# Row gathers, search order and the first value block of a product-key expert kernel

## What is computed

```python
q = (xt @ wq).reshape(T, 8, 2, 128)
s = einsum('thpd,hpnd->thpn', q, keys)           # 8 heads, 2 halves, 128 keys
v1, i1 = top_k(s[:, :, 0], 16); v2, i2 = top_k(s[:, :, 1], 16)
sc, ci = top_k(all 256 sums v1 + v2, 16)         # 16 of 16384 experts per head
e = i1[ci // 16] * 128 + i2[ci % 16]; g = softmax(sc)
act = gelu(sum_d x[d] * u_tab[e, d])
out = sum over the 128 chosen e of g * act * v_tab[e]
```

## Time and profile before

| | us |
|---|---|
| median of 3 runs | 2322.4 |
| the profiled execution, its own time | 2329.6 |
| its span, first to last instruction | 2327.8 |
| PE busy | 2186.6 (94%) |
| first score block / first value block starts | 756.6 / 1616.0 |

### The profile page before, as it was taken

The page is one execution under the profiler, slowest core; times in us unless marked ns, Lnnn a source line. Parts: engine busy times, 40 slices in busy tenths (PEclk is TensorE's granted clock), DMA queues, the critical chain, the costliest instruction groups (busy, mean ns, idle before and its releaser), DMA issues.

```text
span 2327.8 us, 34710 instructions
## 1 busy us (share of the span) xinstructions
PE 2186.6 (94%) x11688; PEld 1949.6 (84%) x11688; DVE 1631.0 (70%) x3216; ACT 798.9 (34%) x1028; POOL 771.6 (33%) x522
## 2 busy tenths in 40 slices
PE   5899997999999999898699999997999999999998
PEld 2789996999999878787588989886888888888887
DVE  4449998041343597979878888886777777777785
ACT  1435554112332322222244545443222222222222
POOL 1223322323123567776522222221232222322340
PEclk8999998999799999999899999998999999999997
DMA  8212223334322578787567777776998999889991
GB/s 347 82 56 62 64 64 110 110 102 145 123 64 64 169 240 258 234 270 232 176 215 293 278 278 274 290 276 200 302 307 303 307 309 310 302 307 309 312 319 71
DMA packets 167190, 496.80 MB, mean 213 GB/s; under 512 B 16576, under 2 KB 74304, under 8 KB 165568
## 3 DMA queue, kind: packets, MB, share of 16 engines
q1 hardware_dynamic: 101584, 268.72, 34.9%
q0 software_dynamic: 46080, 167.79, 21.1%
q10 hardware_dynamic: 19440, 59.25, 6.4%
HBM read 433.83 MB, written 61.87 MB: 213 GB/s over the span
## 4 chain that ended last, share of the span: by engine, by line
PE 71%; DVE 12%; issue 8%; DMA 5%; POOL 3%; ACT 2%; SPq 0%; ACTq 0%; POOLq 0%; DVEq 0%
PE P L754 29%; PE P L513 19%; PE P L682 12%; PE P L705 4%; PE P L531 3%; DVE rows L1392 2%; DMA rows<-in_u_tab,Eg 2%; POOL rows L458 2%; DMA gel_scratch<-gel 2%; PE P L599 1%; POOL wLo L442 1%; DMA tb<-in_posT 1%; PE P L726 1%; DVE oh L1421 1%; DVE keysel L1430 1%
## 5 line engine op out<-in xcount | busy, mean ns | idle before, releaser
L778 ACT ACTIVATE wHi<-raw 128x1024 fp32r<-128x1024 f32 x330 | 346.2, 1049 | 1295.2 <-PE P L754 471.7
L682 PE MATMUL P<-hHi,wHi 128*128 128x480 f32 x1024 | 400.4, 391 | 48.4 <-POOL wLo L442 44.6
L754 PE MATMUL P<-wfHi,wHi 128*128 128x480 f32 x1024 | 392.0, 383 | 14.0 <-DVE wfLo L1559 14.0
L682 PE MATMUL P<-hLo,wHi 128*128 128x480 f32 x1024 | 393.2, 384 | 0.0
L682 PE MATMUL P<-hHi,wLo 128*128 128x480 f32 x1024 | 393.0, 384 | 0.0
L754 PE MATMUL P<-wfLo,wHi 128*128 128x480 f32 x1024 | 391.8, 383 | 0.0
L754 PE MATMUL P<-wfHi,wLo 128*128 128x480 f32 x1024 | 391.7, 382 | 0.0
L1491 DVE TENSOR_TENSOR wLo<-raw,wHi 128x1024 fp32r<-128x1024 f32 x188 | 230.2, 1225 | 181.0 <-ACT wHi L778 179.0
L436 POOL TENSOR_TENSOR wLo<-raw,wHi 128x1024 fp32r<-128x1024 f32 (+1 forms) x76 | 186.4, 2454 | 511.9 <-ACT wHi L778 511.7
L458 POOL DMA_INDIRECT rows<-in_v_tab,Eg x160 | 177.4, 1109 | 483.6 <-DVE accB L1531 232.3
L458 POOL DMA_INDIRECT rows<-in_u_tab,Eg x160 | 193.0, 1206 | 393.5 <-DVE rows L1392 359.6
(11 more groups left out here) (216 smaller groups left out, 3164.7 us busy)
## 6 DMA issues: line engine op xcount, KB each, us to landing
raw<-in_ublk SPq DMA_DIRECT2D x128, 512.0 KB, 4.2
raw<-in_v_tab SPq DMA_DIRECT2D x128, 512.0 KB, 5.6
raw<-in_wblk SPq DMA_DIRECT2D x104, 512.0 KB, 3.7
gel_scratch<-gel ACTq DMA_DIRECT2D x128, 240.0 KB, 3.5
gsr<-gel_scratch SPq DMA_DIRECT2D x128, 240.0 KB, 5.7
gate_scratch<-stage ACTq DMA_DIRECT2D x6, 4096.0 KB, 14.5
gates<-gate_scratch SPq DMA_DIRECT2D x32, 768.0 KB, 7.3
modraw<-in_wblk SPq DMA_DIRECT2D x12, 512.0 KB, 13.1
```

The costliest lines, as they stand in the source:

```text
L682: last = nc.tensor.matmul(P[0][:, j % 2, 0:TD], w_[:, j % 2, k * 128:(k + 1) * 128], x_[:, k, C0:T], start=(k == 0 and a == 0 and b == 0), ...
L754: last = nc.tensor.matmul(P[k // 2][:, k % 2, 0:TD], w_[:, j % 2, k * 128:(k + 1) * 128], x_[:, j % 2, :], start=(first and a == 0 and b = ...
L778: return nc.scalar.activation(out, in_, f, **kw)
```

## The change

It has five parts.

1. The ring of `u_tab` rows has eight buffers: four `rows` as before and four `rowsX` in the memory of `x`. So `x` is stored to DRAM (`x_park`, in the unused eighth part of `gate_scratch`) by SP ahead of the load of query block 6, and loaded back to a new place `x2` by SP half-way through the value blocks; the last steps use `x2`. The `v_tab` gathers keep four buffers.
2. `D1` is 88: 88 gathers are spread over the 60 blocks 8 to 67, written out; the other 72 come in loops of 24 with row numbers copied 12 at a time.
3. DVE's units: tiles 0 to 2 of heads 0 to 5, then (6,0), (6,1), (7,0), (6,2), (7,1), (7,2), then tiles 3 and 4. `select` works on some of the heads of a tile (tile 0: heads 0 to 3, 4 to 6, 7; others 0 to 3 and 4 to 7) with up to five dots inside. 70 dots may be done before softmax, 12 after it, 6 around the first `low` on DVE.
4. PE waits for softmax and transposes behind block 63, ACT's exp stands ahead of its last eight blocks.
5. `gsr` and the first buffer of `gates4`, `wf`, `wfHi` and `wfLo` lie in the memory of `x`; SP loads `gsr` and gates of the first value blocks once all `u_tab` dots are done. The gate products of the last score block come ahead of its scores, ACT rounds the first `wf` ahead of the last GELU, and the first value block starts with chunks 4 to 7.

The diff, cut to its core:

```diff
-UR = 4
+UR, VR = 8, 4
-D1 = 80
+D1 = 88
     x = sb("x", [128, KC, T])
     free_to(0)
+    rowsX = sb("rowsX", [128, UR - VR, D])
+    free_to(0)
+    gsr = sb("gsr", [128, 4, TD])
+    gates4 = [sb("gates4a", [128, 6, 4, 64])]
+    wf, wfHi, wfLo = (...)
...
+            if (name, m) == ("wq", 6):
+                sp_.wait_ge(s["norm_t"], 2 * KC)
+                sp_.dma_start(x_park, x[:, :, :]).then_inc(s["x_pk"], 16)
...
-        for j in range(RAW):
-            value_block(0, j)
+        sp_.wait_ge(s["row_free"], NG + UR)
+        sp_.wait_ge(s["x_pk"], 16)
         for h in range(2):
-            sp_.wait_ge(gel_st[h], 16 * NE // 2)
             sp_.wait_ge(gate_st[h], 16 * 3)
+            sp_.wait_ge(gel_st[h], 16 * 2)
         gate_rows(0, 0, 0)
         for j in range(RAW):
             gate_block(0, j)
+        for j in range(RAW):
+            value_block(0, j)
+        sp_.wait_ge(s["prod_done"], P_V)
         gate_rows(0, 1, 4)
+        for h in range(2):
+            sp_.wait_ge(gel_st[h], 16 * NE // 2)
...
+        with sp_.Fori(1, NE // 16) as i:
+            eight_blocks(i)
+        sp_.dma_start(x2[:, :, :], x_park).then_inc(s["x_up"], 16)
+        with sp_.Fori(NE // 16, NE // 8) as i:
+            eight_blocks(i)
...
+        for b in range(U1 - 8):
+            low(0, 0, 8 + b)
+            for g in range(b * D1 // (U1 - 8), (b + 1) * D1 // (U1 - 8)):
+                if g % 8 == 0:
+                    indices(0, 0, g, g // 8 % 2, 0, 8, g // 8 + 1)
+                gather(0, 0, g + 1, g % UR, g // 8 % 2, g % 8, u_tab)
...
-        with pe.Fori(0, U1 // 4) as i:
+        with pe.Fori(0, U1 // 4 - 1) as i:
...
         last.then_inc(s["tr2_done"], 1)
+        for j in range(4):
+            expert_scores(U1 // 4 - 1, 0, j)
...
+        gates_of(U2 // 4 - 1, 3)
+        expert_scores(U2 // 4 - 1, U1, 3)
...
-        with act.Fori(1, U1 // 4 - 1) as i:
+        with act.Fori(1, U1 // 4 - 2) as i:
...
+            if last:
+                value_halves(0, 0)
+                gelu_out(ib, U1, j)
...
-        units = [(h, t) for h in range(4) for t in range(2)] + [(h, 0) for h in range(4, HEADS)]
-        units += [(h, 1) for h in range(4, HEADS)] + [(h, t) for t in range(2, NT) for h in range(HEADS)]
+        units = [(h, t) for h in range(6) for t in range(3)] + [(6, 0), (6, 1), (7, 0), (6, 2), (7, 1), (7, 2)]
+        units += [(h, t) for t in range(3, NT) for h in range(HEADS)]
...
             search(n, unit, before)
-                early_dots(3)
+            early_dots(2)
+            if before is not None:
+                hb, tb_ = before
+                parts = {3: [(0, 4)], 6: [(4, 7)], 7: [(7, 8)]} if tb_ == 0 else {7: [(0, 4), (4, 8)]} if tb_ < 3 else {
+                    3: [(0, 4)], 7: [(4, 8)]}
+                for h0, h1 in parts.get(hb, ()):
+                    select(tb_, h0, h1)
+                    selects += 1
+                if hb == HEADS - 1 and tb_ < 2:
+                    row_numbers(tb_, selects)
+                    if tb_ == 0:
+                        dve.sem_inc(s["row_free"], UR)
+                        dotted[1] = D1 - 18
+                elif n < len(units):
+                    early_dots(1)
...
                         ).then_inc(s["sm_ready"], 1)
-        early_dots(4)
+        dotted[1] = D1 - 6
+        early_dots(D1 - 6)
```

More of the change, by code:

```diff
@@ L453, in indices, with gather @@
                 hold(pool, s["eg_ready"], i * per + count, s["pool_held"])
-        def gather(i, per, seq, buf, at, tab):
-            hold(pool, s["row_free"], i * per + (seq + 1), s["pool_held"])
-            pool.indirect_dma_start(out=rows[:, seq % UR, :], out_offset=None, in_=tab,
+        def gather(i, per, free, n, buf, at, tab):
+            hold(pool, s["row_free"], i * per + free, s["pool_held"])
+            pool.indirect_dma_start(out=row(n), out_offset=None, in_=tab,
                                     in_offset=bass.IndirectOffsetOnAxis(ap=Eg[:, buf, at:at + 1], axis=0)
-                                    ).then_inc(row_ld[seq % UR], 16)
@@ L462, in gather_u @@
-        def gather_u(i, base, g):
-            if g % 8 == 0:
-                indices(i, 2, i * 16 + (base + g), g // 8, 0, 8, (base + g) // 8 + 1)
-            gather(i, 16, base + g, g // 8, g % 8, u_tab)
-        with pool.Fori(0, 2) as i:
-            for j in range(4):
-                low(i, 4, j)
+                                    ).then_inc(row_ld[n], 16)
+        for b in range(8):
+            low(0, 0, b)
+        pool.wait_ge(s["x_pk"], 16)
         pool.wait_ge(s["e_ready"], 1)
@@ L485, in _ @@
+        pool.wait_ge(s["e_ready"], 2)
+        with pool.Fori(0, (NG - D1) // 24) as i:
+            for g in range(24):
+                if g % 12 == 0:
+                    indices(i, 2, i * 24 + (D1 + g), (D1 // 8 + g // 12) % 2, 0, 12, D1 // 8 + g // 12 + 1)
+                gather(i, 24, D1 + g + 1, (D1 + g) % UR, (D1 // 8 + g // 12) % 2, g % 12, u_tab)
         with pool.Fori(0, NE // 16) as i:
             for half in range(2):
-                indices(i, 4, i * 16 + half * 8, half, 0, 8, 0, last=False)
@@ L750, in values @@
             pe.wait_ge(s["wlo_ready"], i * 4 + (j + 1))
-            for k in range(KC):
+            for k in ((4, 5, 6, 7, 2, 3, 0, 1) if first else range(KC)):
+                if first and k == 2:
+                    pe.wait_ge(s["bank_free"], 2 + 2 * U2)
+                if first and k == 0:
+                    pe.wait_ge(s["gel_free"], 2 + NE)
                 for a, (w_, xs) in enumerate(((wHi, (wfHi, wfLo)), (wLo, (wfHi,)))):
@@ L1034, in _, with value_halves @@
         actf(SC[:, :], SCm, ACT.Exp).then_inc(s["exp_ready"], 1)
-        for j in range(4):
-            gelu_out(U1 // 4 - 1, 0, j)
+        for j in range(8):
+            gelu_out(U1 // 4 - 2 + j // 4, 0, j % 4)
+        def value_halves(i, j):
+            if not (isinstance(i, int) and j < 2):
+                w_hi(i * 4 + (P_V + j), j, i + B_V // 4, j % 2)
+            act.wait_ge(s["wf_ready"], i * 4 + (j + 1))
+            act.wait_ge(s["prod_done"], i * 4 + (P_V + j - 1))
+            actf(wfHi[j % 2][:, :], wf[j % 2][:, :], ACT.Copy).then_inc(s["whi_ready"], 1)
         def gate_block(ib, j, half, off):
-            gelu_out(ib, U1, j)
+            last = isinstance(ib, int) and ib * 4 + j == U2 - 1
+            if not last:
+                gelu_out(ib, U1, j)
             for q in range(2):
@@ L1070, in _ @@
         actf(wgt[:, :], actv[:, :], ACT.Gelu_apprx_tanh).then_inc(s["gel_ready"], 1)
[L1072 to L1079 removed]
+        for j in range(1, 4):
             value_halves(0, j)
```

236 lines of the change are left out of this document (120 added, 116 removed).

## The result

The changed kernel takes 2283.07 us (median of 4 runs, 2281.97 to 2288.36) against 2323.09 for the kernel before (4 runs): a ratio of 0.9823, 95% interval 0.9806 to 0.9841. It is faster by 40 us; the forecast was 2270. In a later comparison on another chip it took 2280.52 (5 runs), ratio 0.9807 (0.9779 to 0.9836).

The account below looks back on a forecast made before the run. PE, busy 94% of the span, bounds the kernel, so only holes and slow clock can be won. Gains 42 + 10.5 = 52 us make the profiled 2329.6 2277.6; less 7.3 to the median, 2270; own range 2260 to 2284, widened 2253 to 2294.

Parts of the forecast that it names:

- (a): Query products, new search order: 21 units done instead of 12, first dot at 804, DVE's 24 us idle costing PE nothing.
- (c): End of the first 68 expert blocks: a hole of about 18 us stays, at block 62 instead of 66.
- (b): Blocks 8 to 67: gathers pace dots; DVE needs 260 us, POOL 4.6 per block; blocks 19 to 57 without holes.
- third rival: POOL becomes the bound of blocks 8 to 67 at 6.8 us per block: 40 us slower, 2363; chance 0.04.
- (d): Start of block 68: taken at 1134 us, a gain of 42 us, bounds 34 and 64.
- (e): Parking x, one store and one load of 2.6 MB on SP's queue: 0 us, bounds 0 and 10.
- (f): Second stage, 60 blocks with 72 dots instead of 80: change of 0 us, between -2 and +2.
- (g): First value block, with early loads and the last block's gates first: gain 10.5 us, bounds 4 and 14.
- The second: DVE lags more: holes of 3 to 5 us at selections, some 30 at block 62; about 2294; chance 0.17.
- The first: The hole at block 62 is absent or small: 2248 us, half-way 2259; chance 0.13.
- The fourth: x's load delays the value stage or DVE's order gives back POOL's win: within 7 us of before; chance 0.03.
- the 64 us: First 68 expert blocks of the kernel before: they need 355 us and took 419.1, so 64 us are lost.

Follow-up runs that it names:

- The run with the old order: Changed kernel with the last score block's scores ahead of its gate products and its GELU ahead of the gate copies: 2282.74 us, ratio 0.9821.
- the late dots: Changed kernel with early dots allowed only once tile 1 is selected, not tile 0: 2264.89 us, ratio 0.9732.
- Interleaved tiles: Kernel before with its six wf tiles ordered wf, wfHi, wfLo of buffer a, then those of b, in the old place: 2320.56 us.

## Why the prediction was right, and where its steps were not

The time lay 13 us above the forecast, 1 us inside its own range of 2260 to 2284, and the direction was right. The place and the releasers of the large hole were right; one term was much too small, what paces the dots was wrong, and one gain was missing. That the time still fell into the narrow range is luck: without the 9 us that the value stage gained by the new addresses, which I had not seen coming, it would have been 2292.

Of the 13 us, some 5 are the sum (52 forecast, 47.6 between the two profiles). The other 8 are the base: I took the whole gain off the median, but read it from an execution 7 us above that median, and its first score stage was 7 us longer than that of its repetition. What of the gain was scatter can't be told exactly from two executions.

**(a) Search order: right on the start, wrong on the price.** The first dot came at 803.7 (I kept 804), behind an idle DVE (20.9 us; I wrote some 24). But I wrote that this idling "costs PE nothing". It costs nothing at that moment and all of it at the end: with two searches and tile 1's selection put into it, `S` came 22.1 us earlier and the time fell by 18 us. I had shown in (c) that DVE's last work sets the hole, and then didn't carry an idle stretch of the same engine to it.

**(b) The failed step: DVE's sum, and that gathers pace the dots.** I put DVE at 260 us from 804, "so it could end near 1064 unpaced", and let gathers pace it. It took 301 us (803.7 to 1105.3), and after about 825 it hardly waited for rows at all. Of the 41 us, 27 are the selections (107 us for eight halves against 80), 8 waits for rows, 7 the dots (70 at 1.63 on the mean against 1.53), and the searches, with the small gaps between instructions, were 1 less. Hence dot 69 ended at 1065.8 and not at 1050. With an engine that is nearly full, its sum is the path, and what it idles earlier is lost.
That no hole of 3 to 5 us is left at selections was right. The run with four buffers shows that it is not the eight that did it: its longest wait before the last hole is 2.9 us.
POOL's `low` fell from 2.68 to 2.60 us on the mean, with more dots beside it, so the third rival is refuted and DVE is the one that mostly waits. The Trainium skill (SBUF — State Buffer, "Who interferes with whom") names the instructions which can contend with GpSimd for a shared pair of ports, casts among them. The trace agrees: the cast of 128 columns above took 2.45 us, from 1069.97 to 1072.42, beside this `low` of POOL, against 0.29 for 256 columns with POOL shut out.

```profile
1069.94 2.39 POOL L467 TENSOR_TENSOR wLo<-raw,wHi 128x1024 fp32r<-128x1024 f32 x1 [0.73 <-ACT wHi L811]
```

Such waits may be a part of the 27 us of selections; how these divide over waits and over the cut in two was not tried.

**(c) The hole at block 62: right in place and cause, 24.6 us instead of 18.** Gather 78, exp and PE stand as written. From the end of dot 69 to the end of `S` I counted 39.5 us; it took 40.3 (1065.8 to 1106.1). Two errors nearly cancel in it: the half selection beside POOL took 12.8 us instead of 10.5, the searches 18.4 instead of 19.8. The hole ended 17.5 us later than I had it, at 1114.8 instead of 1097.3: 15.8 because dot 69 was late, 0.8 in these 40.3, and 0.9 between the end of `S` and the first product. It is only 6.3 us longer (24.6 against 18.3), since PE too was late: it had finished block 61 at 1090.2 (1114.8 - 24.6), where I had 1079. The eight small waits of blocks 8 to 61 make 5.2 us (29.8 - 24.6), and the rest is what each costs in restart and clock: after the wait of 1.9 us at 836.9 eight products came 0.40 us apart instead of 0.22. Behind the large hole, block 62 took 8.1 us instead of 5.2: 2.9 us of slow clock, where I had 1.6.

**(d) Block 68.** I had it start at 1134 (1131.6 and 2 for one-hots); it started at 1150.2. The gain up to there was 25.2 us against this profile of before and 18.1 against its repetition, below my lower bound of 34 either way. That bound stretched only "the sum of (c)" by 15%; it should have stretched the sum of (b), the 260 us of DVE. The wait for the first one-hots is 1.4 us and stands behind block 68's scores, so it shows at block 69.

**(e) Parking `x`: right.** The load took 12.5 us (I had 9.9 and bounded a delay of 10), the gate loads beside it 9.5 and 11.5, and PE had no hole in the value stage. My bounds asked what the moved memory could cost; that it could speed products up was not among them, and this missing term is 9 us: the value operands came to lie at other addresses. The 10.6 us split into 1.8 of clock in the first block (6.98 us before, 5.19 now) and 8.9 of pace over the other 127.

**(f) Second stage: nearly right.** I had 0, between -2 and +2. PE's waits for one-hots from block 69 to the value start (1184.5 to 1616 us before, 1159.2 to 1580 after) were

```profile
PE P L705 <- DVE ohA L1503: 3.8, 4, 1.5
...
PE P L724 <- DVE ohA L1551: 4.6, 4, 3.1
```

and 3.5 of the 4.6 us are the two waits of step (g). So 2.7 us of the 12.0 were gained inside the stage.

**(g) First value block: right, some 11 us against 10.5** (the 9.3 that are left of the 12.0 ahead of the first value product, and 1.8 behind it). I had the waits for one-hots at 3.9 us and they were 3.5; the slice 1570 to 1575 shows the granted clock of 0.66 that they leave, the small cost I counted at 1.4. The run with the old order shows that the gates need not go first for most of this.

**The rivals.** The second (DVE lags more, 30 us of hole, gain 25 to 30) had its mechanism half right: selections were dearer by a third, the hole was 24.6 us, and the gain of the stage was 18 to 25, but there were no holes of 3 to 5 us at selections. The first (no hole) is what the late dots bring about. The fourth is refuted by the ratio. What hid the miss in the sum is the pace of the value stage.

## What to carry to other kernels

When one engine's last piece of work sets a hole, add up all that it does from the last time it idles, and count every idle stretch of it before that point at full price: work that needs nothing from outside (here two searches and a selection) goes in front of the first wait for data. A deeper ring doesn't make a late engine earlier (`S` came 351 us behind the first block with four buffers and 349 with eight); it decides how far the others run before they stop, which was worth 20 us here only together with the new order. So undo the order and the ring one at a time before crediting either. After any change of the memory plan compare the pace of a stage that was full before and after, product by product. And before a loss is read from one execution, look at a second one of the same kernel: here 7 of the 64 us were gone in it.

## What the runs showed of the hardware that I had not expected

The pace of these matmuls depends on where tiles lie in memory: 24 products of 480 columns took 5.28 us with `wfHi` and `wfLo` 32 bytes off a multiple of 64, and 5.23 and 5.19 in turn on multiples of 64, with nothing else changed but 32 bytes of padding, which moved `gsr`, `gates4` and `wf` along (1.3% over the value stage). PE never stood idle and its granted clock was 1.00 in both. It is not the whole rule. In the change only the first buffer lies on a multiple of 64 (5.18 us); the second is 32 bytes off, and its blocks run in 5.24 us, hardly slower than the aligned ones. Interleaved tiles, all 32 bytes off, ran in 5.25 and 5.27, and the score products, whose `hHi` is 32 bytes off, run in 5.20. What exactly is hit, PE's operand or the reads and writes that DVE and ACT do at the same time, stays open.

Second, the stage of the first 68 blocks, where POOL, ACT and DVE wait for each other, differs by 10 us between executions of kernels that are the same there (409.0 to 419.1 us to block 68; 419.1 and 412.0 for the unchanged kernel), while the value stage of those with the old pace repeats within 0.6 us (680.0 to 680.5). A single profile can't decide a question of that size in the first of them.
